# Two of each expert's six weight loads issued by ScalarE's queue, four by SyncE's

## The reference

```python
def run_block(args):
    toks, e = args
    xb = h_pad[toks]
    gu = xb @ w_gu[e] + b_gu[e]
    g, u = gu[:, :D_EXPERT], gu[:, D_EXPERT:]
    g = jnp.minimum(g, SWIGLU_LIMIT)
    u = jnp.clip(u, -SWIGLU_LIMIT, SWIGLU_LIMIT)
    act = (u + 1.0) * (g * jax.nn.sigmoid(SWIGLU_ALPHA * g))
    return act @ w_dn[e] + b_dn[e]
```

## Time and profile before

| | us |
|---|---|
| median of 3 runs | 1620.03 |
| lowest and highest | 1618.67, 1624.53 |
| the profiled execution's own time | 1622.31 |
| its span, first to last instruction | 1620.5 |
| TensorE busy in the span | 1533.4 (95%) |
| VectorE, ScalarE busy | 458.9, 278.4 |
| moved by DMA | 515.65 MB, 318 GB/s on average |

### The profile page before, as it was taken

The page is one execution under the profiler, slowest core; times in us unless marked ns, Lnnn a source line. Parts: engine busy times, 40 slices in busy tenths (PEclk is TensorE's granted clock), DMA queues, the critical chain, the costliest instruction groups (busy, mean ns, idle before and its releaser), DMA issues.

```text
span 1620.5 us, 18431 instructions
## 1 busy us (share of the span) xinstructions
PE 1533.4 (95%) x7491; PEld 871.9 (54%) x7491; DVE 458.9 (28%) x983; ACT 278.4 (17%) x552; POOL 21.3 (1%) x42
## 2 busy tenths in 40 slices
PE   7889999999999999999999999999999998998997
PEld 6768787786877888743333333333333333233232
DVE  2434636613346381221211121121112111111111
ACT  1324114324232531120000000000000000000000
POOL 4000000000000000000000000000000000000000
PEclk9989999999999999999999999999999999999999
DMA  9761876447332442789999999999999999999996
GB/s 256 172 220 69 306 257 226 157 152 251 135 108 102 142 144 104 318 350 426 427 426 428 427 427 427 428 428 428 428 427 427 428 427 427 427 427 426 427 427 285
DMA packets 84330, 515.65 MB, mean 318 GB/s; under 512 B 5573, under 2 KB 8933, under 8 KB 59697
## 3 DMA queue, kind: packets, MB, share of 16 engines
q1 hardware_dynamic: 81744, 511.29, 77.9%
q0 software_dynamic: 2240, 3.02, 1.8%
q10 hardware_dynamic: 288, 0.53, 0.1%
HBM read 511.15 MB, written 3.15 MB: 317 GB/s over the span
## 4 chain that ended last, share of the span: by engine, by line
PE 79%; DMA 14%; DVE 3%; ACT 2%; issue 1%; another core or an unknown queue 1%; ACTq 0%; SPq 0%; DVEq 0%
PE psum L511 27%; PE psum L1177 20%; PE psum L1274 11%; DMA ring<-in_w_gu 9%; DMA w_down<-in_w_gu 4%; PE psum L520 4%; PE psum L1155 4%; PE psum L1164 2%; PE psum L1122 2%; PE psum L551 1%; PE psum L576 1%; PE psum L1262 1%; DVE hidden L2265 1%; PE psum L545 1%
## 5 line engine op out<-in xcount | busy, mean ns | idle before, releaser
L511 PE MATMUL psum<-spare,ring 128*128 128x256 f32 x1504 | 334.1, 382 | 2.9 <-ACT spare L1489 2.6
L511 PEld LDWEIGHTS psum<-spare,ring 128*128 128x128 f32 x1504 | 284.2, 191 | 50.4 <-issue 10.3
L1177 PE MATMUL psum<-ring,hg 128*64 128x512 f32 x1040 | 233.4, 596 | 7.5 <-DMA ring<-in_w_gu 7.5
L1177 PEld LDWEIGHTS psum<-ring,hg 128*64 128x64 f32 x1040 | 71.0, 137 | 156.5 <-issue 140.0
L1177 PE MATMUL psum<-w_down,hg 128*64 128x512 f32 x656 | 146.3, 596 | 4.7 <-DMA w_down<-in_w_gu 4.7
L2256 DVE TENSOR_SCALAR gu<-psum 128x512 f32<-128x512 f32 x32 | 22.1, 692 | 326.0 <-PE psum L1177 326.0
L2268 DVE TENSOR_TENSOR o_slot<-psum,gain_rows 128x512 f32<-128x512 f32 x32 | 22.1, 692 | 319.0 <-PE psum L1274 319.0
L1177 PEld LDWEIGHTS psum<-w_down,hg 128*64 128x64 f32 x656 | 44.8, 137 | 97.6 <-issue 88.7
L1274 PE MATMUL psum<-w_down,hiddenT 128*64 128x512 f32 x352 | 78.0, 595 | 9.4 <-ACT hiddenT L1731 7.2
L1274 PE MATMUL psum<-ring,hiddenT 128*64 128x512 f32 x352 | 78.0, 594 | 8.3 <-issue 8.3
L1725 ACT ACTIVATE putT<-psum 128x256 f32<-128x256 f32 x32 | 12.3, 384 | 380.9 <-PE psum L1184 380.8
(11 more groups left out here) (417 smaller groups left out, 1445.5 us busy)
## 6 DMA issues: line engine op xcount, KB each, us to landing
ring<-in_w_gu SPq DMA_DIRECT2D x65, 2048.0 KB, 28.0
w_down<-in_w_gu SPq DMA_DIRECT2D x41, 2048.0 KB, 28.1
ring<-in_w_in SPq DMA_DIRECT2D x24, 2048.0 KB, 9.5
w_down<-in_w_dn SPq DMA_DIRECT2D x22, 2048.0 KB, 28.6
ring<-in_w_dn SPq DMA_DIRECT2D x22, 2048.0 KB, 31.5
ring<-in_w_ada SPq DMA_DIRECT2D x12, 2048.0 KB, 8.1
spare<-in_w_gu SPq DMA_DIRECT2D x11, 2048.0 KB, 28.1
nine<-in_w_gu SPq DMA_DIRECT2D x11, 2048.0 KB, 29.6
```

The costliest lines, as they stand in the source:

```text
L511: mm = pe.matmul(bank[0:m, c * T:(c + 1) * T], w[:, k, c0 + c * P:c0 + c * P + m], src[:, k, :], start=(i == 0), stop=(i == k_n - 1))
L1177: mm = pe.matmul(psum[half * CAP:(half + 1) * CAP, loop_bank(4 + part), :], hg[:, k, side, :], w[:, c0:c0 + 512], start=False, stop=(k == ...
```

## The change

ScalarE issues the loads of (n+1, 5) and (n+2, 0) after its copy to `hiddenT` of expert n, without a further wait: by then the products that used their slots' old tiles are done. SyncE keeps j = 1 to 4, with the waits that it had. `load` now takes the engine that issues, and moves out to where both can call it. ScalarE's loop, two experts long before, becomes six long, since slots repeat with six experts. For the last experts, where there is no n+2 or n+1, `loads` is 1 or 0. The leftover experts' loop keeps its loads on SyncE, with a function `expert_more` without them.

```diff
+    def load(eng, i, m, e, j):
+
+        slot, _ = expert_slot_of(i, m, j)
+        tile, loaded, _ = weight_slot(slot)
...
+        eng.dma_start(tile.rearrange("p (k n) -> p k n", k=k), src.rearrange("e p k n -> (e p) k n"))\
+            .then_inc(loaded, 16)
...
         def load_after(i, m, n, j):
-            if j == 0:
-                sp.wait_ge(ev("gu_done"), 2 * n - 2)
-            elif j < 3:
+            if j < 3:
                 sp.wait_ge(ev(f"down_done{j - 1}"), n - 1)
             else:
                 sp.wait_ge(ev("gu_used"), 3 * n + j - 5)
-            load(i, m, n, j)
+            load(sp, i, m, n, j)
...
-        for j in range(3, 6):
+        for j in range(3, 5):
             load_after(0, 1, 1, j)
         with sp.Fori(0, SIXES) as i:
             for m in range(2, 8):
-                for j in range(6):
+                for j in range(1, 5):
                     load_after(i, m, 6 * i + m, j)
...
-        def expert(n, side, gather_after=None):
+        def expert(i, m, side, gather_after=None, loads=2):
+
+            n = 6 * i + m
...
             act.activation(hiddenT[:, :, :], psum[:, loop_bank(6), :].rearrange("p (i s) -> p i s", i=4), ACT.Copy)\
                 .then_inc(ev("hiddenT"), 1)
+            if loads > 0:
+                load(act, i, m + 1, n + 1, 5)
+            if loads > 1:
+                load(act, i, m + 2, n + 2, 0)
...
-        expert(0, 0)
-        expert(1, 1, gather_after=3)
-        with act.Fori(1, PAIRS - 1) as i:
-            expert(2 * i, 0)
-            expert(2 * i + 1, 1, gather_after=2 * i + 3)
-        expert(NE - 2, 0)
-        expert(NE - 1, 1)
+        expert(0, 0, 0)
+        expert(0, 1, 1, gather_after=3)
+        with act.Fori(0, SIXES - 1) as i:
+            for m in range(2, 8, 2):
+                expert(i, m, 0)
+                expert(i, m + 1, 1, gather_after=6 * i + m + 3)
+        i = SIXES - 1
+        for m in range(2, 6, 2):
+            expert(i, m, 0)
+            expert(i, m + 1, 1, gather_after=6 * i + m + 3)
+        expert(i, 6, 0, loads=1)
+        expert(i, 7, 1, loads=0)
```

More of the change, by code:

```diff
@@ L399, in expert_slot_of @@
         return t % SLOTS, 4 * i + t // SLOTS
+    def load(eng, i, m, e, j):
+        slot, _ = expert_slot_of(i, m, j)
+        tile, loaded, _ = weight_slot(slot)
+        if j < 4:
+            src = w_gu[bass.ds(e, 1), :, 2 * j:2 * j + 2, :]
+            k = 2
+        else:
+            src = w_dn[bass.ds(e, 1), :, j - 4, :, :]
+            k = 4
+        eng.dma_start(tile.rearrange("p (k n) -> p k n", k=k), src.rearrange("e p k n -> (e p) k n"))\
+            .then_inc(loaded, 16)
     banks = {}
@@ L1359, in load_after @@
                 sp.wait_ge(ev("gu_used"), 3 * n + j - 5)
-            load(i, m, n, j)
+            load(sp, i, m, n, j)
         for j in range(2):
             sp.wait_ge(*slot_last[occupants[j]])
-            load(0, 0, 0, j)
+            load(sp, 0, 0, 0, j)
         sp.wait_ge(ev("mixed"), 4)
-        load(0, 0, 0, 4)
-        load(0, 0, 0, 5)
-        load(0, 1, 1, 0)
+        load(sp, 0, 0, 0, 4)
+        load(sp, 0, 0, 0, 5)
+        load(sp, 0, 1, 1, 0)
         for j in range(2, 4):
             sp.wait_ge(*slot_last[occupants[j]])
-            load(0, 0, 0, j)
+            load(sp, 0, 0, 0, j)
         product(sp, "ht11")
-        load(0, 1, 1, 1)
+        load(sp, 0, 1, 1, 1)
         sp.wait_ge(ev("residual"), 4)
-        load(0, 1, 1, 2)
-        for j in range(3, 6):
+        load(sp, 0, 1, 1, 2)
+        for j in range(3, 5):
             load_after(0, 1, 1, j)
@@ L1389, in _ @@
                     for j in range(6):
-                        load(i, None, e, j)
+                        load(sp, i, None, e, j)
             sp.nop()
@@ L1732, in expert, with expert_more @@
                 .then_inc(ev("hiddenT"), 1)
+            if loads > 0:
+                load(act, i, m + 1, n + 1, 5)
+            if loads > 1:
+                load(act, i, m + 2, n + 2, 0)
+        def expert_more(n, side):
+            act.wait_ge(ev("turned"), n + 1)
+            act.activation(putT[:, side, :], psum[:, loop_bank(7), 0:T], ACT.Copy).then_inc(ev("putT"), 1)
+            act.wait_ge(ev("g_in"), n + 1)
+            act.activation(hidden[:, 0, :], gu[:, 0, :], ACT.Sigmoid, scale=1.702).then_inc(ev("g_sig"), 1)
+            act.wait_ge(ev("hidden_turned"), n + 1)
+            act.activation(hiddenT[:, :, :], psum[:, loop_bank(6), :].rearrange("p (i s) -> p i s", i=4), ACT.Copy)\
+                .then_inc(ev("hiddenT"), 1)
         gathered(1, first_bank=6)
@@ L1751, in _ @@
                     gathered(2 * i + 2 * PAIRS + 1, 1)
-                    expert(i + NE, 0)
+                    expert_more(i + NE, 0)
                 act.wait_ge(ev("added"), first + TOGETHER + NE - 1)
```

## The result

The changed kernel is slower: 1631.4 us in the median of 11 runs (1626.6 to 1638.0), against 1622.4 of the kernel before in 11 runs (1614.6 to 1628.6). The ratio is 1.0059, with a 95% interval of 1.0037 to 1.0080, which is 9.6 us (6.0 to 13.0). The forecast was 13.2 us.

A forecast was written before the change was run, and what follows sets the result against it. The prediction took the DMA engines' loads to set the pace: 6.2 us idle plus 9.8 overtaking less 2.8 gained back is 13.2 us, added to the 1620.0 median for 1633 us, range 1623 to 1645.

The forecast's parts named there:

- What bounds the kernel: Experts' stage: from 1301.6 us the DMA engines set the pace, 4.91 us a load; idle time after 700 is paid in full.
- The gap at the start: First expert: DMA engines idle from 715.0 to 721.2 until ScalarE's first pair is issued behind its copy; 6.2 us.
- Overtaking: Loop: ScalarE's pair lands ahead of the awaited (n+1, 3), two loads or 9.8 us, lost once; bounds 0 and 9.8.
- T + 35.2: Loop: end of ScalarE's pair, T being SyncE's issue of (n+1, 3); TensorE wants that tile at T + 36.5.
- 0.8 + 9.8: ScalarE's first load of a pair: 0.8 us from issue to first data, then 9.8 us at half rate; landing about 11.
- the half share: Loop: two large streams on two queues take half the DMA engines each, so ScalarE's pair needs 19.6 us.
- the first wait near 1000: Sign in the profile: TensorE's first wait for a load comes eleven experts sooner, near 1000 in place of 1300 us.
- Gained back: Last round: only (31, 5) overtakes (31, 3), which lands before TensorE wants it; 2.8 us gained back.
- Loads served by time of issue: Rival: nothing overtakes in the loop, only the idle 6.2 us remain, 1626; 0.15 together with a fuller rate.
- A rate changed by the second queue: Rivals, experts' stage: fuller rate 1623.5 (within 0.15), 2% less 1645 (within 0.16), faster by 3.5% more (0.06).
- the 10 ns a packet: Time beside each packet's transfer; a second queue filling it would raise the rate 1.6%, to 434 GB/s, 9.7 us back.
- ScalarE's share under a third: Rival: with a quarter share ScalarE's pair needs 39.3 us and (n+2, 0) is awaited, 1643; 0.16 together with lost rate.

The follow-up runs named there:

- e2: Kernel before, all loads on SyncE, but each expert's j = 5 waits for the previous expert's copy to hiddenT; ratio 1.0058, stage 925.7 us.
- e3: Kernel before, all loads on SyncE, but only (1, 5) waits for the first copy to hiddenT, (2, 0) behind it; ratio 1.0023, stage 925.3 us.
- e5: Changed kernel, but SyncE issues the first pair and ScalarE each later pair behind a wait for gu_done; ratio 1.0040, stage 928.1 us.
- e4: Changed kernel, but ScalarE issues its pair after the sigmoid behind a wait for gu_done, not behind the copy to hiddenT; ratio 1.0045, stage 928.3 us.
- e7: Kernel before, but ScalarE carries only (n+2, 0), issued when its slot is free, first pair on SyncE; ratio 1.0000, stage 923.0 us.
- e1: Changed kernel, but the first pair, (1, 5) and (2, 0), is issued by SyncE as before; ratio 1.0059, stage 934.4 us.

## Why the prediction was right

**What bounds the kernel.** Confirmed: idle time of the DMA engines put in by e2 and e3 comes out at the end nearly one for one (5.7 and 6.4 us' worth in, 5.5 and 6.0 us out).

**The gap at the start.** Right in place, 5.1 us' worth in place of 6.2. The step took the load to be issued behind the end of the copy; the rows show it issued as the copy begins (714.38 and 714.37), one copy of 0.6 us earlier. The loads ahead of the gap ended about 0.8 us later in the stage than summed (710.6 - 695.5 against 715.0 - 700.8). The issues took 0.4 us each, less than the 0.63 that the prediction allowed.

**Overtaking.** Right in kind, and all but 1.3 of the 11.6 us by which (29, 3) is late in e5. In the changed kernel (29, 3) is 14.0 us late, and less the gap that is 8.9 in place of 9.8. The step that was mis-sized is when the pair is through: the prediction has both loads through at T + 35.2, before TensorE wants the tile. (30, 0) lands at 1551.2, which is T + 38.8 and 4.0 us behind (29, 3). The first load of a pair takes 14 us, not 11. The prediction's 0.8 + 9.8 counts up to the last byte; a load that meets idle engines, (1, 3) from 704.44 in the kernel before, takes 7.2 us to land with 4.9 of transfer, so 2.3 come on top of the transfer there, 1.5 more than the 0.8. In e4 and e5, where the pair is issued 3 us sooner after (29, 3), the full 9.8 and 10.3 are lost. The working also has the half share right, and the first wait near 1000 (1017).

**Gained back.** 3.2 us in place of 2.8, with no wait for (31, 3), as forecast.

The stage lost 5.1 + 8.9 - 3.2 = 10.8 us in place of 13.2, and the ratio says 9.6 (6.0 to 13.0). The forecast of 1633 stood on the 1620.0 of three runs; with eleven the kernel before is at 1622.4.

**The rivals.** Loads served by time of issue: out, since (29, 5) is issued 13.9 us behind (29, 3) and lands 5.9 us ahead of it, and since in e7, with no load late and some 0.9 us idle, (29, 3) still comes 6.3 us late. And e2, with one queue and every pair late, costs its gap alone. A rate changed by the second queue: out in both directions, 425 to 428 GB/s past the first 55 us in the windows of all eight variants, so the 10 ns a packet are not to be had. ScalarE's share under a third: out, it is a half. The rule of the Trainium skill ("DMA: Bandwidth & Descriptors", Issuing engines are not separate DMA queues) that transfers begun by several engines only interleave agrees with these rates. The Trainium skill's turn packet by packet ("DMA: Bandwidth & Descriptors", Queues, rings and completion order) agrees with the half share, 9.8 us for the second load of the pair.

**What the prediction missed** is that the gap is not tied to the start: e1 shows it again 29.5 us later, at the second pair. Past the first 55 us the changed kernel, e1 and e2, whose pairs are all late, run at 427 and 428 GB/s. The prediction also takes two whole loads of overtaking for each round, and in the changed kernel the second load passes wholly in some rounds only.

## What to carry to other kernels

When TensorE eats up a stock of prefetched tiles and the DMA engines are full from then on, look for two things only: idle time of the DMA engines anywhere since the stage began, and the order in which tiles land against the order in which they are wanted. One queue in the order of use was the fastest of the orders tried here; a second queue on the same engines brought no bandwidth (425 to 428 GB/s with either) and let later tiles pass earlier ones. Issuing late cost nothing as long as loads were queued (e2 against e3, 0.4 us), so a kernel's first two or three rounds have to be checked apart from its loop.

## What the runs showed of the hardware that I had not expected

A load on ScalarE's queue, when SyncE's queue is full, lands 13.7 to 14.0 us after its issue in the median in all the two-queue kernels, also when it is alone on its queue. A second one behind it needs 9.8 us more, half the rate. Half the rate from the start would give an estimated 12.1: 9.8 of transfer and the 2.3 that a load into idle engines takes beyond its own transfer, read from (1, 3) of the kernel before, in the DMA view from 704.3 to 704.6 us:

```profile
ring<-in_w_gu SPq DMA_DIRECT2D x1, 2048.0 KB, 7.2
```

So 1.6 to 1.9 us are left, and no run shows what they are.

ScalarE issues a transfer that stands behind a copy when the copy starts, not when it ends. In the changed kernel that is 714.38 against 714.37, and once 1499.73 against 1499.78, while the copy before it was still running; in e1 once 1560.52 against 1560.57.

A wait of TensorE for a load can bring its granted clock down to 0.50. Each of the waits of 3.8 us and more in these kernels was followed by slow products, as the 4.5 us in e1; none of up to 1.9 us was; and of those from 2.1 to 3.1 us some were and some were not. The changed kernel's 2.50 us are followed by 5.35 us for sixteen product instructions (the row at 1017.05), with 0.50 from 1018 to 1020. TensorE's timeline of e4:

```profile
1082.90 3.65 PE L1190 MATMUL psum<-ring,hg 128*64 128x512 f32 x16 [2.52 <-DMA ring<-in_w_gu]
1200.57 5.35 PE L1190 MATMUL psum<-w_down,hg 128*64 128x512 f32 x16 [2.44 <-DMA w_down<-in_w_gu]
1259.41 3.65 PE L1190 MATMUL psum<-ring,hg 128*64 128x512 f32 x16 [0.79 <-DMA ring<-in_w_gu]
```

The kernel before waits nearly as long in all (14.4 us against 16.8), but never more than 1.3 us at a time, and its products keep their 3.65 us. While the loads set the pace the slow products are hidden: in e4 the 1.7 us that they take longer come off the next wait, which is 0.79 us. At the last wait of e1 nothing takes them up, and they cost 2.5 us.
